# Extra 128x512 matmuls on TensorE around the attention heads of a two-block kernel

## What is computed

```
z = einsum('bsd,de->bse', h, w_in)            # 1024 -> 3072
ya = rglru_group(a_x, a_y, ...)               # linear recurrence, width 256
yb = hgrn2_group(b_q, b_f, b_i, b_g, ...)     # gated linear attention, 4 heads of 64
yc = moba_group(c_q, c_k, c_v)                # 8 heads of 64, causal softmax with a slope
y = concatenate([rms_norm(ya), yb, rms_norm(yc)])
x = x + einsum('bse,ed->bsd', y, w_out)
...
```

## Time and profile before

| | |
|---|---|
| median of 3 timed runs | 1432.66 us (1431.24 to 1433.78) |
| profiled execution: its own time | 1428.76 us |
| profiled execution: span, first to last instruction | 1426.9 us |
| mean granted TensorE clock | 0.978 |
| TensorE matmuls, busy | 1380.6 us (97%) |
| TensorE weight loads, busy | 1228.5 us (86%) |
| GpSimd busy | 1056.3 us (74%) |
| VectorE busy | 763.6 us (54%) |
| ScalarE busy | 714.1 us (50%) |
| DMA, mean | 184 GB/s |

### The profile page before, as it was taken

The page is one execution under the profiler, slowest core; times in us unless marked ns, Lnnn a source line. Parts: engine busy times, 40 slices in busy tenths (PEclk is TensorE's granted clock), DMA queues, the critical chain, the costliest instruction groups (busy, mean ns, idle before and its releaser), DMA issues.

```text
span 1426.9 us, 29009 instructions
## 1 busy us (share of the span) xinstructions
PE 1380.6 (97%) x9762; PEld 1228.5 (86%) x9762; DVE 763.6 (54%) x1620; ACT 714.1 (50%) x1128; POOL 1056.3 (74%) x469
## 2 busy tenths in 40 slices
PE   6999999999999998899999999999999999999997
PEld 6978899997877787799999999999977777788885
DVE  4665533334338715439992166666678888611113
ACT  5634555555355444425556544434445555556663
POOL 6751788887679787568888877777767777788885
PEclk9995999999999999999999999999999999999998
DMA  7650777774535448445555554444444444465552
GB/s 263 215 190 11 252 268 287 268 278 161 197 133 188 142 157 303 160 161 163 182 186 177 177 170 156 160 162 155 155 152 169 164 162 164 166 246 194 196 193 92
DMA packets 72651, 263.02 MB, mean 184 GB/s; under 512 B 8208, under 2 KB 9104, under 8 KB 72224
## 3 DMA queue, kind: packets, MB, share of 16 engines
q1 hardware_dynamic: 72608, 262.46, 53.6%
HBM read 259.81 MB, written 2.62 MB: 184 GB/s over the span
## 4 chain that ended last, share of the span: by engine, by line
PE 41%; POOL 30%; issue 21%; DVE 4%; DMA 2%; ACT 1%; POOLq 1%; SPq 0%; ACTq 0%; DVEq 0%
POOL wlo L426 30%; PE bank L826 8%; PE bank L827 8%; PE bank L828 8%; PE bank L809 4%; PE bank L811 4%; PE bank L810 4%; DMA raw<-stream 2%; DVE arena L1613 1%; PE bank L899 1%; PE bank L919 0%; PE bank L936 0%; PE bank L935 0%; DMA arena<-ada 0%; POOLq L425 0%
## 5 line engine op out<-in xcount | busy, mean ns | idle before, releaser
L426 POOL TENSOR_TENSOR wlo<-raw,whi 128x1024 fp32r<-128x1024 f32 x432 | 1042.1, 2423 | 293.4 <-ACT whi L485 289.7
L485 ACT ACTIVATE whi<-raw 128x1024 fp32r<-128x1024 f32 x432 | 454.0, 1052 | 202.7 <-PE bank L828 117.1
L809 PE MATMUL bank<-xh,whi 128*128 128x256 f32 x1600 | 460.8, 288 | 8.2 <-DVE xl L1214 5.1
L810 PE MATMUL bank<-xl,whi 128*128 128x256 f32 x1600 | 454.3, 284 | 0.0
L811 PE MATMUL bank<-xh,wlo 128*128 128x256 f32 x1600 | 454.1, 284 | 0.0
L809 PEld LDWEIGHTS bank<-xh,whi 128*128 128x128 f32 x1600 | 308.6, 193 | 12.7 <-issue 5.8
L810 PEld LDWEIGHTS bank<-xl,whi 128*128 128x128 f32 x1600 | 308.8, 193 | 1.2
L811 PEld LDWEIGHTS bank<-xh,wlo 128*128 128x128 f32 x1600 | 308.4, 193 | 0.0
L826 PE MATMUL bank<-whi,uh 128*128 128x512 f32 x640 | 255.0, 398 | 3.0 <-DVE ul L1807 3.0
L827 PE MATMUL bank<-wlo,uh 128*128 128x512 f32 x640 | 249.7, 390 | 0.0
L828 PE MATMUL bank<-whi,ul 128*128 128x512 f32 x640 | 249.2, 389 | 0.0
(11 more groups left out here) (281 smaller groups left out, 1302.9 us busy)
## 6 DMA issues: line engine op xcount, KB each, us to landing
raw<-stream SPq DMA_DIRECT2D x432, 512.0 KB, 3.3
arena<-ada SPq DMA_DIRECT2D x48, 512.0 KB, 4.4
arena<-rows SPq DMA_DIRECT2D x5, 512.0 KB, 8.9
xs<-x SPq DMA_DIRECT2D x2, 512.0 KB, 4.5
arena<-rows SPq DMA_DIRECT2D x1, 1024.0 KB, 5.4
x_spill<-xs SPq DMA_DIRECT2D x1, 1024.0 KB, 6.3
xs<-x_spill SPq DMA_DIRECT2D x1, 1024.0 KB, 5.9
out<-arena SPq DMA_DIRECT2D x2, 512.0 KB, 2.6
```

The costliest lines, as they stand in the source:

```text
L426: nc.gpsimd.tensor_tensor(wlo[:, slot, :], raw[:, slot, :], whi[:, slot, :].bitcast(F32), ALU.subtract).then_inc(lo_done, 1)
L485: nc.scalar.activation(whi[:, slot, :], raw[:, slot, :], ACT.Copy).then_inc(hi_done, 1)
L809: nc.tensor.matmul(dst, h_, xh[:, k, :], start=(k == 0), stop=False)
L810: nc.tensor.matmul(dst, h_, xl[:, k, :], start=False, stop=False)
```

## The change

A helper issues matmuls of the tile `xh[:, 4:6, :]` (512 columns, fp32r) with a stationary operand from `xh` as well, into all of bank 6. Each starts and ends its own sum, waits for no semaphore and signals none. Six are issued after the last `level_scores` and ahead of the wait for `in_m`, and three at the head of each of the eight turns of the loop over the heads: 30 matmuls, each with its weight load. Nothing is removed or moved.

```diff
+            def keep_busy(count):
+
+                for _ in range(count):
+                    nc.tensor.matmul(bank[6][:, :], xh[:, 4, 0:P], xh[:, 4:6, :], start=True, stop=True)
+
+            keep_busy(6)
             pe.wait_ge(S("in_m"), 4)
             a_scores(0)
             pe.wait_ge(S("ones_set"), 1)
@@
             a_scores(1)
             for h in range(8):
+                keep_busy(3)
                 a_turn(h)
                 if h + 2 < 8:
                     a_scores(h + 2)
```

## The result

The changed kernel took 1421.44 us (median of 7 runs, 1418.33 to 1423.59), the kernel before 1431.50 us (median of 7 runs, 1427.32 to 1433.78). The ratio is 0.9927, with a 95% interval of 0.9911 to 0.9942.

The account below looks back on a forecast made before the run. The prediction took TensorE at half clock, 30.7 us in the attention part, as the bound there. With the clock held its steps summed to -7.1 us: 1432.66 - 7.1 = 1425.6 us, range 1421.5 to 1435.

Parts of the forecast that it names:

- The likeliest case: Attention part: the clock holds at 1.00 throughout, -7.1 us, 1422 to 1429 us; chance 0.68.
- four rivals: Half clock all the same (0.10), clock falling on the way (0.12), transposes not counting (0.04), time taken back (0.06).
- First scores: Start of the attention part: the six fillers run from 102.28 to 103.66 us, delaying the first scores by 0.49 us.
- To the end of the third scores: Running sum after second scores, head 0's fillers and transposes, and third scores at full clock: -0.59 us.
- `hg_values`: 24 instructions after the third scores: 5.31 us becomes 2.85 at full clock, bringing the running sum to -3.05 us.
- Heads 1 to 5: Loop over heads: 3.69 us becomes 2.84 with fillers; head 5, with four more transposes, 4.54 becomes 2.84 + 0.49.
- Heads 6 and 7: Last two heads: head 6 goes from 2.48 to 2.42 us, head 7 from 2.18 to 2.80 us (+0.62).
- Sum: All steps of the attention part added up for a clock that holds: -7.1 us.
- with the fillers the part looks more like the first: Attention part likened to 160.16 to 166.40 us, where the clock stayed at 1.00, rather than 580.00 to 583.41 us, where it fell.
- The rival of the clock falling in `hg_values`: Clock falls on the way, each later head costing 1.28 us more; 1438.6 to about 1426 us; chance 0.12.
- The rival that transposes don't count: Clock falls where transposes pile up, in heads 5 and 6: 1430.1 us; chance 0.04.
- The take-back in VectorE and ScalarE: Clock holds, but VectorE and ScalarE pace the heads or the gain is lost behind: 1428.4 to 1432 us; chance 0.06.

Follow-up runs that it names:

- the two later comparisons: The changed kernel timed again against the kernel before: 1423.11 us, ratio 0.9957; then side by side on one chip: 1423.21 us, ratio 0.9954.
- the three other places: Kernel with one filler for each head, plus fillers at three places of half clock behind the attention part: 1419.28 us, ratio 0.9938 to the kernel before.

## Why the prediction was right and where it was wrong

The mechanism held: the clock at 1.00 from the first scores to the output projection, TensorE as what paces the part, fillers at 0.23 to 0.25 us each on its path. The likeliest case came in, and none of the four rivals. What failed is the start of the sum, and with it the range, which had no term for the start. By the steps of the prediction:

- **First scores**: forecast +0.49. They began at 103.63 against 103.17 us, +0.46, or +0.7 from the start of the part's work, which was 0.25 us earlier. The six took 1.59 us, where 1.38 were counted.
- **To the end of the third scores**: forecast -0.59, measured 108.87 against 109.53 us, so -0.66, or -0.41 without the 0.25 from ahead.
- **`hg_values`**: forecast 2.85 us, measured 111.69 - 108.87 = 2.82.
- **Heads 1 to 5**: forecast 2.84 us for a head, measured 2.73. The steps at full clock had been read where TensorE was waiting for something: 0.48 for the first score product is 0.42 in the loop, 0.43 for the first value product is 0.36, and three transposes are 0.33 instead of 0.37. The fillers are 0.75, not 0.69. Over five heads this is 0.6 us.
- **Heads 6 and 7**: forecast 2.42 + 2.80 = 5.2 us, measured 130.40 - 125.82 = 4.6: without scores, the values take 0.17 + 0.22 + 0.22.
- **Sum**: forecast -7.1, measured -8.1. This term was mis-sized by 1.0 us.
- **The time**: here is the step that failed. The sum was worked out on the profiled execution, which took 1428.76 us, and was then moved up by 3.9 us to the median of three runs, "1432.66 - 7.1". Those three were a high draw: all seven of the same comparison have a median of 1431.50 us, and the 84 executions of the kernel before on record 1430.2. The range had 1.6 us for hand-overs and 1.7 for each spell of half clock, but nothing for the start, although the prediction itself had a distance of 3.9 us between two readings of the same kernel.

The miss of 4.2 us splits into 1.2 us of start (1432.66 against 1431.50) and 3.0 us of gain (10.1 against 7.1). Of the gain, 1.0 us is the mis-sized part. The other 2.0 us show in no trace: the profiled pair differs by 7.7 us. Most likely they are a draw as well, since the two later comparisons gave 5.7 and 6.2 us. So the part's gain is 8.1 us in every trace, and the whole kernel's lies between 5.7 and 10.1 us in three comparisons; the intervals of the first and the later two barely overlap, and what makes the difference is open. Profiled against profiled, the forecast was 1421.7 us and the measurement 1421.03, and this closeness is partly luck: the part gained 1.0 us more than was worked out, and 0.7 us was given back behind it, which the sum had put at nothing.

The argument for the clock, "with the fillers the part looks more like the first", came to the right answer with half the reason. It treated the six and the three as one measure. The six decide: without them the clock falls and the heads' fillers turn into a loss (1436.47 us), and with them alone it held in the trace (1420.29 us). Three in place of one cost 2.9 us in the part. What the heads' fillers buy is not shown: with none, one execution of six took 1425.62 us at 0.981, with one the six lie within 4.6 us, all at 0.986 or more, and that is too few to call it evenness. The rival of the clock falling in `hg_values`, where no filler stands, is answered by the same kernels: it held there in every trace that had six wide fillers, or the twelve transposes in their place, ahead of the first scores. The rival that transposes don't count fell with the kernel that had only transposes as fillers. The take-back in VectorE and ScalarE did not appear with three fillers; it is what limits the gain with one or none, where the chain goes over line 590.

What stays open: whether rows count beside columns, what happened in the single longer executions with no filler in the heads, and whether fewer or narrower fillers than six of 512 columns ahead of the first scores would do, which was not tried.

## What to carry to other kernels

When TensorE's clock falls in a part with narrow work, look at the few microseconds ahead of the fall: here, filling that one spot with wide matmuls that nobody waits for kept the full clock for the next 25 us, and once it had fallen, three wide matmuls for each head did not lift it. Fillers are paid in full where TensorE sets the pace, so put in the fewest that hold. As many fillers of two columns did not hold it, though TensorE was recorded as busy. Half clock costs time only where TensorE is what the rest waits for; look at the chain before filling such a place, as the 2.1 us lost at the first of the three other places show. For an effect below 1%, take the start of the sum from many executions, give it a term in the range, and compare the length of the changed part in several traces: it repeated within 0.1 us here, while the medians' differences ran from 5.7 to 10.1 us.

## What the runs showed of the hardware that was not expected

- Two-column matmuls with full weight loads, TensorE recorded busy for 3.86 of 4.00 us, and the clock fell all the same, for 44.4 us.
- The same heads kept the level that they began at: with three fillers they held 1.00 when they began at it (14.10 us) and stayed at 0.50 when they began at that (37.6 us). Without fillers it was the same, in one trace and in four.
- With transposes of the identity (float32) as the only fillers, the clock held at 1.00 for 27.90 us.
- Raising the mean clock from 0.986 to 0.992 behind the attention part brought 1.5 us between the medians, inside the uncertainty. At one of the three places the fillers cost 2.1 us on TensorE's path and the way behind them took 12.5 us with and without them.
